# Second norm reordered around its stored half, a written-out convolution projection, and decay gates computed inside a gate projection

## What is computed

```
# first block
h = rms_norm(x, norm_w);  proj = h @ w_in
q, k, v = silu(centred depthwise conv, 5 taps, of proj's first 1536 columns)
beta = sigmoid(proj's beta logits);  g = -exp(a_log) * softplus(decay logits + dt_bias)
dn = gated delta rule, forward and backward, in chunks of 64 (cumulative sums of g)
sw = windowed attention with sinks (rotary q, k)
x = x + concat(rms_norm(dn) * silu(z), sw * silu(z2)) @ w_out
# second block
h = rms_norm(x, norm_g_2);  proj = h @ w_in_2      # 48 columns of weight tiles
attention over 9 chunks of 64, gated causal conv, merge, output projection, final rms_norm
```

## Time and profile before

| what | value |
|---|---|
| median of 3 runs | 3504.36 us (3499.03 to 3515.44) |
| profiled execution | 3508.2 us, span of its trace 3506.3 us |
| mean granted TensorE clock | 0.934 of full speed |
| busy share of the span | PE 88%, PE weight loads 73%, DVE 52%, ACT 37%, POOL 19% |
| DMA | 423.12 MB, mean 121 GB/s |

### The profile page before, as it was taken

One profiled execution on the slowest core, in us unless ns is written; L12 is line 12 of the kernel. 1 busy time (PEld: TensorE's weight loads), 2 busy tenths in 40 slices (PEclk: granted clock), 3 DMA queues, 4 the chain that ended last, 5 costly groups with the idle time before them and its releaser, 6 DMA issues. The chain is left out here.

```text
span 3506.3 us, 62044 instructions
## 1 busy us (share of the span) xinstructions
PE 3096.0 (88%) x23542; PEld 2574.2 (73%) x23542; DVE 1813.7 (52%) x3185; ACT 1287.7 (37%) x2648; POOL 674.1 (19%) x567
## 2 busy tenths in 40 slices
PE   5998798894999998969927999999999979949799
PEld 5777797684999995648725888878888747738687
DVE  5554443072455554655454577565676445543333
ACT  4222343152444445851042332442323357720132
POOL 0000000051233221023243223243232111120000
PEclk8999899996899998979958999999999989979899
DMA  3211675253233333226444322353323260054543
GB/s 115 72 54 66 226 235 175 74 157 109 90 127 132 126 123 95 74 89 206 151 146 129 109 72 76 112 173 114 93 72 101 90 188 16 15 204 157 202 145 119
DMA packets 293711, 423.12 MB, mean 121 GB/s; under 512 B 41840, under 2 KB 185072, under 8 KB 288112
## 3 DMA queue, kind: packets, MB, share of 16 engines
q1 hardware_dynamic: 251344, 383.88, 33.2%
q10 hardware_dynamic: 42144, 36.18, 3.2%
HBM read 270.56 MB, written 149.42 MB: 120 GB/s over the span
## 5 line engine op out<-in xcount | busy, mean ns | idle before, releaser
L106 PE MATMUL pj_pp<-h_hi,pj_whi 128*128 128x512 f32 x1344 | 525.5, 391 | 29.5 <-DVE pj_wlo L2762 25.3
L108 PE MATMUL pj_pp<-h_hi,pj_wlo 128*128 128x512 f32 x1344 | 524.6, 390 | 0.0
L107 PE MATMUL pj_pp<-h_lo,pj_whi 128*128 128x512 f32 x1344 | 524.5, 390 | 0.0
L106 PEld LDWEIGHTS pj_pp<-h_hi,pj_whi 128*128 128x128 f32 x1344 | 253.4, 189 | 83.2 <-issue 31.1
L108 PEld LDWEIGHTS pj_pp<-h_hi,pj_wlo 128*128 128x128 f32 x1344 | 253.2, 188 | 53.1
L107 PEld LDWEIGHTS pj_pp<-h_lo,pj_whi 128*128 128x128 f32 x1344 | 253.3, 188 | 52.4
L2699 ACT CAST pj_whi<-pj_raw 128x512 fp32r<-128x512 f32 x240 | 149.0, 622 | 349.5 <-PE pj_pp L108 317.2
L2762 DVE TENSOR_TENSOR pj_wlo<-pj_raw,pj_whi 128x512 fp32r<-128x512 f32 x240 | 228.0, 951 | 86.6 <-ACT pj_whi L2699 78.6
L106 PE MATMUL pc_pp<-h_hi,pc_whi 128*128 128x512 f32 x384 | 154.1, 401 | 20.2 <-DVE pc_wlo L327 20.2
L107 PE MATMUL pc_pp<-h_lo,pc_whi 128*128 128x512 f32 x384 | 153.3, 399 | 0.0
L108 PE MATMUL pc_pp<-h_hi,pc_wlo 128*128 128x512 f32 x384 | 153.1, 399 | 0.0
(11 more groups left out here) (343 smaller groups left out, 7319.1 us busy)
## 6 DMA issues: line engine op xcount, KB each, us to landing
pj_raw<-in_w_second SPq DMA_DIRECT2D x192, 256.0 KB, 2.9
ds_pk<-scratch_pack SPq DMA_DIRECT2D x32, 1280.0 KB, 8.2
scratch_pack<-rp_out SPq DMA_DIRECT2D x32, 512.0 KB, 2.7
scratch_sig_fm<-pj_ob SPq DMA_DIRECT2D x64, 256.0 KB, 2.1
mb_sg<-scratch_sig_fm SPq DMA_DIRECT2D x16, 1024.0 KB, 7.5
scratch_qkv_fm<-pc_acc SPq DMA_DIRECT2D x12, 1024.0 KB, 4.9
rp_fm<-scratch_qkv_fm SPq DMA_DIRECT2D x96, 128.0 KB, 2.8
n_x<-in_x SPq DMA_DIRECT2D x16, 512.0 KB, 4.3
```

What stands on the lines that cost most here:

```text
L106: nc.tensor.matmul(out, ah, bh, start=(first and i == 0), stop=False)
L107: nc.tensor.matmul(out, ah, bl, start=False, stop=False)
L108: mm = nc.tensor.matmul(out, al, bh, start=False, stop=(last and i == n - 1))
```

## The change

Three parts. (1) `project_conv` is written out without loops: weights are loaded three tiles ahead, behind the split that frees their buffer and no longer behind a store; casts and splits of the next weights come right behind the product that frees them; all taps come in one transfer; the last tile goes through copy, convolution, SiLU and store in four column pieces. (2) `project_rows` and `delta_gates` become one function, `gate_rows_decays`: the chain of the decay gates runs on ACT and DVE beside the 16 row tiles, its three small matmuls stand ahead of row tile 4, and its two stores stand behind the 16 row stores. (3) `norm_combine` takes the second half of the rows first (pairs 0 to 3, stored) and the first half last (pairs 4 to 7, rounded into SBUF); each rounding stands behind the next pair's combinations in the ACT, DVE and POOL streams, and SP loads the first unit's four weight quarters behind the last rows, into buffers that are now allocated around both stages. In `project_second` the waits for the two constants stand later.

```diff
 def project_conv(...):
+            def load(n):
+                s = n % 2
+                if n >= 2:
+                    sp.wait_ge(lo_ready[s], n // 2 + START)
+                sp.dma_start(raw[s][:], w_tiles[n]).then_inc(w_in[s], 16)
...
+            load(0)
+            load(1)
+            sp.dma_start(taps[:], conv_w.rearrange("n p t -> p n t")).then_inc(taps_in, 16)
+            load(2)
+            for n in range(LAST):
+                s = n % 2
+                if n + 3 <= LAST:
+                    load(n + 3)
+                sp.wait_ge(silu_done[s], n // 2 + 1 + START)
+                sp.dma_start(out[n], acc[s][:]).then_inc(stored[s], 16)
+            for g, at in enumerate(pieces):
+                sp.wait_ge(piece_silu[g], 1 + START)
+                sp.dma_start(out[LAST][:, at], acc[LAST % 2][:, at]).then_inc(stored[LAST % 2], 16)
...
+                act.wait_ge(product[s], n // 2 + 1 + START)
+                if n + 2 <= LAST:
+                    split_hi(n + 2)
+                nc.scalar.copy(pre[s][:, PAD:PAD + SEQ], pp[s][:]).then_inc(copied[s], 1)
...
+            for n in range(LAST):
+                s = n % 2
+                if n + 2 <= LAST:
+                    split_lo(n + 2)
+                dve.wait_ge(copied[s], n // 2 + 1 + START)
+                dve.wait_ge(stored[s], 16 * (n // 2) + START)
+                convolve(n, slice(0, SEQ), tap_done[s], (n // 2) * DN_TAPS)
...
-def delta_gates(nc, consts, rows, dt_bias, a_log, gates):
+def gate_rows_decays(nc, w_group, hi, lo, out, consts, rows, dt_bias, a_log, gates):
...
+            nc.scalar.activation(ln[:], e[:], ACT.Ln).then_inc(log_ready, 1)
+            for t in range(4):
+                evict(t)
+            act.wait_ge(cum_ready, 1 + START)
...
+                if t == 4:
+                    pe.wait_ge(decay_ready, 1 + START)
+                    for d in range(2):
+                        four = slice(4 * d, 4 * d + 4)
+                        nc.tensor.matmul(cums[:, :, four], tri[:, d, :], g[:, :, four], start=True, stop=True)
+                    nc.tensor.matmul(sums[:, 1, 0:N], tri[:, 2, :], g[:].rearrange("p t g -> p (t g)"), start=True,
+                                     stop=True).then_inc(summed, 1)
...
 def norm_combine(...):
-            return (TILES // 2) * (n // 4) + 4 * e + n % 4
+            return (TILES // 2) * (1 - n // 4) + 4 * e + n % 4
...
-                if n >= DIRECT:
+                if n < DIRECT:
                     s = n % 2
...
+            for r in S:
+                for q in S:
+                    sp.dma_start(w_raw[r][q], w_first[q][:, r * K4W:(r + 1) * K4W, :]).then_inc(w_ahead, 16)
...
+                if n > DIRECT:
+                    round_hi(n - 1)
+            round_hi(PAIRS - 1)
...
+                if n > DIRECT:
+                    low_rest(n - 1)
+            low_rest(PAIRS - 1)
...
+                if n > DIRECT:
+                    rest(n - 1)
+            rest(PAIRS - 1)
...
 def project_second(...):
-            for r, q in ((0, 0), (0, 1), (1, 1), (1, 0)):
-                load_w(r, q, 0)
...
-            dve.wait_ge(const_in, 32 + START)
             for i in range(STEPS):
                 split_lo(i, 0)
+            dve.wait_ge(const_in, 32 + START)
```

More of the change, by code:

```diff
@@ L281, in _ @@
         @block.sync
         def _(sp):
-            def load(j, s):
-                sp.dma_start(raw[s][:], w_tiles[2 * j + s]).then_inc(w_in[s], 16)
-                sp.dma_start(taps[s][:], conv_w[2 * j + s]).then_inc(w_in[s], 16)
-            def step(j, more):
-                for s in range(2):
-                    sp.wait_ge(silu_done[s], j + 1 + START)
-                    sp.dma_start(out[2 * j + s], acc[s][:]).then_inc(stored[s], 16)
-                    if more:
-                        load(j + 1, s)
@@ L294, in _ @@
-            for s in range(2):
-                load(0, s)
-            with sp.Fori(0, N - 1) as j:
-                step(j, True)
-            step(N - 1, False)
-            for s in range(2):
-                sp.wait_ge(stored[s], 16 * N + START)
+            def load(n):
[5 more added lines that the diff above has]
+            load(1)
@@ new lines, in _ @@
+            s = LAST % 2
+            for g in range(GROUPS + 1):
+                if g < GROUPS:
+                    act.wait_ge(piece_product[g], 1 + START)
+                    nc.scalar.copy(pre[s][:, PAD + g * NCOL:PAD + (g + 1) * NCOL],
+                                   pp[s][:, cols[g]]).then_inc(piece_copied[g], 1)
+                if g > 0:
+                    act.wait_ge(piece_tap[g - 1], DN_TAPS + START)
+                    at = pieces[g - 1]
+                    nc.scalar.activation(acc[s][:, at], acc[s][:, at], ACT.Silu).then_inc(piece_silu[g - 1], 1)
@@ new lines, in convolve @@
+            def convolve(n, at, sem, base):
+                s = n % 2
+                nc.vector.tensor_scalar(acc[s][:, at], pre[s][:, at], taps[:, n, 0:1], None, ALU.mult).then_inc(sem, 1)
+                for t in range(1, DN_TAPS):
+                    dve.wait_ge(sem, base + t + START)
+                    nc.vector.scalar_tensor_tensor(out=acc[s][:, at], in0=pre[s][:, at.start + t:at.stop + t],
+                                                   scalar=taps[:, n, t:t + 1], in1=acc[s][:, at], op0=ALU.mult,
+                                                   op1=ALU.add).then_inc(sem, 1)
@@ L354, in _ @@
+            s = LAST % 2
+            dve.wait_ge(stored[s], 16 * (LAST // 2) + START)
+            for g, at in enumerate(pieces):
+                dve.wait_ge(piece_copied[g], 1 + START)
+                convolve(LAST, at, piece_tap[g], 0)
         @block.tensor
         def _(pe):
-            with pe.Fori(0, N) as j:
-                for s in range(2):
-                    pe.wait_ge(lo_ready[s], j + 1 + START)
-                    pe.wait_ge(copied[s], j + START)
-                    feature_tile(nc, pp[s], whi[s], wlo[s], hi, lo).then_inc(product[s], 1)
@@ L794, in _, with evict @@
-            nc.scalar.copy(pk[:, 0, :, G_CUM, :], cum[:, :, 0:4])
-            nc.scalar.copy(pk[:, 1, :, G_CUM, :], cum[:, :, 4:8]).then_inc(act_step, 1)
+            def evict(t):
+                s = t % 2
+                act.wait_ge(product[s], t // 2 + 1 + START)
+                act.wait_ge(stored[s], 16 * (t // 2) + START)
+                nc.scalar.activation(ob[s][:], pp[s][:], ACT.Silu).then_inc(copied[s], 1)
+            for a, ks in enumerate(pieces):
+                act.wait_ge(w_in[a], 16 + START)
+                nc.scalar.copy(whi[:, ks, :], raw[:, ks, :]).then_inc(hi_ready[a], 1)
@@ L797, in _ @@
+            for t in range(4, TILES):
+                evict(t)
         @block.vector
@@ L836, in _ @@
[L836 to L840 removed]
+            for t in range(TILES):
+                s = t % 2
+                at = slice(t * P, (t + 1) * P)
+                if t == 4:
[5 more added lines that the diff above has]
+                                     stop=True).then_inc(summed, 1)
+                pe.wait_ge(copied[s], t // 2 + START)
+                for a, ks in enumerate(pieces):
+                    if t == 0:
+                        pe.wait_ge(lo_ready[a], 1 + START)
+                    mm = split_products(nc, pp[s][:], [(hi[:, k, at], lo[:, k, at], whi[:, k, :], wlo[:, k, :])
+                                                       for k in range(ks.start, ks.stop)], first=(a == 0), last=(a == 3))
+                mm.then_inc(product[s], 1)
```

413 lines of the change are left out of this document (192 added, 221 removed).

## The result

The changed kernel took 3470.9 us (median of 4 executions, 3459.9 to 3472.7) against 3507.9 us for the kernel before beside it, a ratio of 0.9893, 95% interval 0.9867 to 0.9919. That is 37 us gained where 55.6 were forecast, and 3471 us lies above the range. The sign was right, and no rival happened as written: `pc_wlo` no longer stops PE, and the second norm gives 6 us, more than the first rival's 4.

The account below looks back on a forecast made before the run. PE's pace bounds the product stages, so gains lie at seams and stages without large products. 28.7 + 16.8 + 10.1 = 55.6 us off the median 3504.4 gives 3448.8 us; 8 in 10 for 3436 to 3466 us.

Parts of the forecast that it names:

- the first rival: Second norm: POOL and DVE hold each other up, ending at or after 1862; part 3 gives 0 to 4 us; chance 0.13.
- convolution, start and stalls: Convolution projection: earlier weight loads, casts and splits remove five `pc_wlo` waits and their clock loss; gain 20.0 us.
- convolution, tail: Convolution projection's end: last tile in four pieces, 11.0 instead of 19.7 us after PE's last product; gain 8.7 us.
- stage `dg` gone: Decay-gate stage between `pg` and the scan: removed with its barrier, its work moved into `pg`; gain 21.3 us.
- `pg` longer: Gate projection: loses 1.2 us to three small matmuls on PE and 3.3 us to the gates' two stores at its end.
- norm and seam: Second norm and projection start: stored pairs first, weights loaded early; PE starts at 1859.2 instead of 1869.34, gain 10.1 us.
- Such a wait costs twice: Convolution projection: PE stands 2.1 us for `pc_wlo`, then the granted clock is 0.69 in the 5.5 us behind it.
- Part 2's list: Decay gates: first SiLU delay 0, three matmuls 1.2 us, two stores 3.3 us, second table round hidden; net gain 16.8 us.
- 1826 + 25.0 + 5.0 = 1856.: Second norm's end: from pair 5 at 1826, POOL's four remainders, then S2 and S4 of two more pairs.
- my three terms: Seam from norm to projection: stage's end 1.7 us, one cast 0.62 us, one split 0.7 us before PE starts.
- The slower one: Convolution projection: written-out code fetched once each starves PE, giving 3522 us or more; chance 0.02.

Follow-up runs that it names:

- the last one: Kernel with three edits and zero products in the scan's opening, plus one zero product ahead of each of ten level halves: 3451.8 us, ratio 0.985.
- zero products: Matmuls of a zero tile while PE waits; 16 ahead of the rope projection, added to the kernel with all three edits: 3446.5 us, ratio 0.984.
- the Exp edit: Changed kernel with ACT running one Exp of one column at the top of the scan: 3455.4 us, ratio 0.9845.
- all three edits: Changed kernel with early Exp, gates' stores behind the seventh tile's, and the last pair's two POOL remainders on DVE: 3449.8 us, ratio 0.9849.

## Why the prediction missed

Stage by stage, each part's mean with it less its mean without it, over the profiles in which the stage had no further edit (and, for the rope projection, without the last one's 115.0):

| step | forecast, us | measured, us |
|---|---|---|
| convolution, start and stalls | 20.0 | 16.1 |
| convolution, tail | 8.7 | 7.3 |
| stage `dg` gone | 21.3 | 21.4 |
| `pg` longer | -4.5 | -3.4 |
| scan's opening | 0 | -4.6 |
| norm and seam | 10.1 | 6.2 |
| rope projection, clock | 0 | -2.3 |
| scan behind its opening | 0 | -3.9, not settled |
| sum | 55.6 | 36.8 |

The medians gave 37 and 38 us, the ratios 37 and 41. (Convolution in all: 306.1 less 282.7; the opening: 19.1 against 23.7; the norm: 113.1 against 106.9.)

No single step carries the 18.8 us that are missing. The two convolution terms were too large by 5.3 us and part 3's sum by 3.9. The scan's opening lost 4.6 us and two stages of unchanged code lost 6.2, all of which the sum had at nothing. The two gate terms came 1.2 us better than forecast.

- **"Gain: 5 x (47.5 - 43.4) = 20.5 us; I take 20.0."** Right in mechanism, mis-sized: 16.1 us in the mean. The cadence came from one execution, in which each stall also lowered the clock, and for that execution 20 was right. In two of four profiles of that code the clock stayed up, and the stage was 6 us shorter. "Such a wait costs twice" is true of some executions.
- **The tail, 19.7 less 11.0 us.** By one mark it was 20.4 less 12.7, and by the stage's length 7.3 us. The pieces cost what I had worked out (3.55 us against 3.6), and the last SiLU ended 8.5 us behind PE, as forecast (8.9). What I had wrong is the last store of the kernel before: it landed in 3.8 us, and I took 4.9, the median of all twelve. That is 1.1 of the 1.4 us. The stage's exit, 1.8 and 1.9 us from that landing to the next stage's first DMA, stood in neither sum, and falls out of the difference.
- **Part 2's list.** What stood in it came near: the stage, the two stores (3.7 us, forecast 3.3), nothing for the first SiLU, though it was 1.8 us late; the three matmuls cost less than I gave them, since with the stores moved up the stage is as short as before. The step that failed is one that I did not make: what the removed stage left behind. It had left the Exp table, and with it gone the scan has to load that table on its first chain. The experiment with one early Exp brings the 4.6 us back.
- **"1826 + 25.0 + 5.0 = 1856."** The end was 3.4 us later relative to the stage's start. The remainders were cheaper than my 6.2 us (5.70, 4.84, 6.20 and 4.66), but S2 and S4 took 8.0 us for 5.0, since S4 took 2.66 us beside DVE; POOL idled 2.5 us for DVE, since DVE's two row scalings took 6.21 us for 2.48 beside POOL's remainders; and S4 of pair 5 ended 71.7 us behind the stage's first DMA, where 1826 is 70.1. The seam took 4.1 us, where my three terms add up to 3.0 and I wrote 3.2; part of that is DVE's split beside POOL's T1. The Trainium skill's rule of the shared SBUF interfaces (GPSIMD Engine Reference, 1. Specifications) is borne out by 2.66 against 1.27 us. I applied it to the remainders, where it was in my rows, and not to the combinations, where it was not.
- **What hung on nothing.** The rope projection's 2.3 us are for the most part its first products at half clock, which zero products ahead of them take away. Why the clock rises later there in nearly all profiles with earlier stages changed, and in one not, stays open.
- **The scan's rest** ran 486.5 to 505.1 us in the ten profiles without the Exp edit, with half the clock, short rises aside, for some 54 to 84 us behind its start. With the gates' part the mean is 3.9 us longer (six against four), with ranges that overlap. I can't say that the change does it. That it is the clock is read from windows, where long scans have the late rise; two attempts to hold it up there moved it and gave nothing in the total. One thing hints at the missing table here too: with the Exp edit and no zero products in the scan the clock rose to stay after 48, 52 and 56 us and the rest took 481.6, 487.8 and 491.4 us, while of the six profiles with the gates' part and without the Exp edit five rose after 76 to 84 us and took 500.3 to 504.8. Three against six profiles, on different chips, do not show it. Open.
- **The rivals.** The first one's mechanism, POOL and DVE holding each other up, is what happened, at about half its size: the norm's work ended at 103.4 us, between the forecast's 100.05 and the rival's 106 (1862). The slower one (written-out code starves PE) is refuted by the window of 259.6 us without a gap. The range was too narrow because its bounds were those of single rows, and took no account of terms that I had not listed, nor of the spread of one stage between executions.

## What to carry to other kernels

When a stage goes, list what it handed to the next besides data: the activation table that it left loaded, the order in which engines arrive, the clock. A price that has TensorE's clock in it, read from one execution, is one draw; look at a second profile of the same code before subtracting it. And in a sum for a tail, take the price of the very transfer that stands there: the last store landed in 3.8 us, the median of its group was 4.9.

The version with all three edits took 3449.8 us, ratio 0.9849, and 3446.5 us with zero products ahead of the rope projection (0.984). Both ratios lie below the changed kernel's 0.9893 and 0.9883, though the intervals overlap a little. By its marks each edit is worth 3 to 5 us.

## What the hardware showed

- A table load of 1.28 us on the first chain of the scan cost 4.6 us, since the work behind it fell under POOL's: DVE's four multiplications of 128 columns took 4.67 us there, 2.20 us in the kernel before and 1.14 us when they ran ahead of POOL.
- DVE and POOL beside each other, both reading two SBUF tiles, fit a picture in which they take turns and the one that comes later waits: on POOL 512 columns at 2.66 for 1.27 us, 1024 columns at up to 3.99 for 2.33 us; on DVE 1536 columns at 3.97 for 1.92 us.
- Without zero products the scan's opening runs at a granted clock of 0.50 for some 48 to 84 us, short rises aside, a different length in each execution. Two profiles of the changed kernel had 56 and 76 us, and the scan behind its opening took 486.5 and 501.0 us, while executions of one kernel lie some 20 us apart.
- Zero products ahead of a stage's first product raised the clock for it (1.00 instead of 0.50); that stage took 114.5 us, against 117.3 in the same kernel without them and 115.0 at best. In the scan the clock fell to 0.50 in a stretch where PE shows 16.00 of 16.00 us busy.
